# Who asks for an expert's rows: moving 28 row loads from GpSimd to ScalarE's hardware queue

## What is computed

```
scores = sigmoid(t @ w_router); best group of 4; top 2 in it; gates normalised
hidden = silu(t @ w_gate[e]) * (t @ w_up[e])        # per expert e, D_FF 512
out    = sum over the token's 2 experts of gate * (hidden @ w_down[e])
```

## Time and profile before

| | us |
|---|---|
| median of 3 runs | 1522.41 |
| lowest, highest | 1518.6, 1524.04 |
| span of the profiled execution | 1516.7 |
| PE busy in it | 1309.2 (86%) |
| ACT busy in it | 338.1 (22%) |
| POOL busy in it | 165.0 (11%) |

### The profile page before, as it was taken

How to read it: one execution, slowest core, us unless ns; L and a number is a source line. 1 busy time by engine, 2 the same in 40 slices (tenths; PEclk the granted TensorE clock), 3 DMA queues, 4 the chain that set the end, 5 groups by cost and what they waited for, 6 DMA issues and landing times.

```text
span 1516.7 us, 38874 instructions
## 1 busy us (share of the span) xinstructions
PE 1309.2 (86%) x16856; PEld 913.1 (60%) x16856; DVE 521.0 (34%) x1144; ACT 338.1 (22%) x671; POOL 165.0 (11%) x238
## 2 busy tenths in 40 slices
PE   5989999989998988899877669888999888998672
PEld 2448844468888457798444334445664678974441
DVE  1324444145556734011101053457555431111003
ACT  2223221143223131000000033433452300010001
POOL 2003310024333001000000030010000010000001
PEclk8999999999999989899999879987979899999997
DMA  9841159831001175899999882134314469999995
GB/s 397 304 154 59 59 202 314 298 151 59 25 37 58 56 288 195 308 386 395 385 398 415 358 296 89 78 121 173 111 56 167 177 250 331 399 393 399 391 426 191
DMA packets 42105, 354.68 MB, mean 234 GB/s; under 512 B 5707, under 2 KB 10651, under 8 KB 23664
## 3 DMA queue, kind: packets, MB, share of 16 engines
q1 hardware_dynamic: 21456, 302.11, 50.7%
q0 software_dynamic: 8704, 28.53, 5.6%
q10 hardware_dynamic: 11808, 22.03, 4.4%
HBM read 321.63 MB, written 31.01 MB: 233 GB/s over the span
## 4 chain that ended last, share of the span: by engine, by line
PE 65%; DMA 17%; DVE 7%; issue 7%; ACT 3%; POOL 1%; SPq 0%; ACTq 0%; POOLq 0%; DVEq 0%
PE PB L688 59%; DMA arena<-in_w_moe 7%; PE PB L691 6%; DMA ring<-in_w_moe 4%; DVE arena L2010 3%; DMA dispatched<-arena,rows_i 2%; DMA ring<-in_w_mod 2%; ACT arena L1540 1%; DMA arena<-dispatched 1%; DVE small L2023 1%; DMA expert_out<-arena 1%; POOL dispatched L631 1%; DVE arena L2017 1%; DVE x L2010 0%; DVE arena L2014 0%
## 5 line engine op out<-in xcount | busy, mean ns | idle before, releaser
L688 PE MATMUL PB<-arena 64*64 64x64 f32 (+6 forms) x9756 | 489.6, 294 | 48.6 <-DMA arena<-in_w_moe 30.0
L688 PEld LDWEIGHTS PB<-arena 64*64 64x64 f32 (+3 forms) x9756 | 399.8, 129 | 133.9 <-issue 69.7
L688 PE MATMUL PB<-ring,hT 128*128 128x512 f32 (+1 forms) x720 | 313.8, 591 | 7.2 <-DVE hT L2013 3.6
L688 PEld LDWEIGHTS PB<-ring,hT 128*128 128x128 f32 x720 | 137.1, 193 | 167.0 <-issue 162.4
L688 PE MATMUL PB<-ring,arena 128*32 128x256 f32 (+2 forms) x3456 | 195.3, 380 | 33.7 <-DMA ring<-in_w_moe 31.0
L688 PEld LDWEIGHTS PB<-ring,arena 128*32 128x32 f32 x3456 | 147.8, 110 | 73.0 <-issue 24.8
L1540 ACT ACTIVATE arena<-PB 128x256 f32<-128x256 f32 (+3 forms) x217 | 106.6, 491 | 331.1 <-PE PB L688 277.5
L691 PE MATMUL PB<-cst,arena 128*128 128x128 f32 (+2 forms) x758 | 118.6, 298 | 52.3 <-ACT arena L1540 17.9
L691 PEld LDWEIGHTS PB<-cst,arena 128*128 128x128 f32 (+2 forms) x758 | 91.1, 157 | 98.6 <-issue 57.9
L2431 DVE TENSOR_TENSOR arena<-arena,PB 128x256 f32<-128x256 f32 (+1 forms) x32 | 15.1, 471 | 300.9 <-PE PB L688 287.7
L688 PE MATMUL PB<-ring,scT 128*32 128x512 f32 x384 | 60.8, 753 | 21.6 <-DMA ring<-in_w_mod 16.0
(11 more groups left out here) (149 smaller groups left out, 928.9 us busy)
## 6 DMA issues: line engine op xcount, KB each, us to landing
arena<-in_w_moe SPq DMA_DIRECT2D x50, 2048.0 KB, 16.5
ring<-in_w_moe SPq DMA_DIRECT2D x46, 2048.0 KB, 14.5
ring<-in_w_mod SPq DMA_DIRECT2D x24, 2048.0 KB, 8.9
ring<-in_w_mix SPq DMA_DIRECT2D x22, 2048.0 KB, 8.6
dispatched<-gate ACTq DMA_DIRECT2D x1, 8320.0 KB, 50.4
arena<-dispatched POOLq DMA_DIRECT2D x20, 256.0 KB, 9.2
expert_out<-gate ACTq DMA_DIRECT2D x1, 3456.0 KB, 22.1
expert_out<-arena ACTq DMA_DIRECT2D x12, 288.0 KB, 8.7
```

The costliest lines, as they stand in the source:

```text
L688: return nc.tensor.matmul(out, lhsT, rhs, start=start, stop=stop, **k)
```

## The change

GpSimd no longer asks for the experts' rows; its loops at L636 to L644 are gone, and after the scatter its next instruction is the gather behind the stage. ACT asks for them. It waits for `dispatched` after `silu(0)`, asks for the rows of experts 2 and 3, and goes on with `rows_copy(1)`. From then on, the request for expert `c+3` stands right behind `rows_copy(c+1)` and ahead of `store(c-1)`. It has no wait of its own: `rows_copy(c+1)` has waited until PE had turned over the rows of `c+1`, which lay in the same buffer. ACT's first loop (the experts with 96 rows) is written out, which the sizes of the requests need.

```
-                L = base_loop[l]
-                with pool.Fori(1, FULL // 2) as i:
-                    for b in range(2):
-                        pool.wait_ge(*steps_of(L, "xT_p", i, b - 2))
-                        pool.dma_start(xb[0:CAP, b, :], Xd[...CAP rows...]).then_inc(x_land[b], 16)
-                with pool.Fori(FULL // 2, half) as i:
-                    ... the same with SMALL
@@ ACT, experts(l)
                 rows_copy(L, None, 0, 0)
                 nc.scalar.activation(xT[:, 0, 4 * CAP:8 * CAP], PB[:, 1, 0:4 * CAP], ACT.Copy).then_inc(L["S"]["xT_v"], 1)
                 silu(L, None, 0, 0, CAP)
+                def load(b, row, cap):
+                    act.dma_start(xb[0:cap, b, :], Xd[row, :]).then_inc(x_land[b], 16)
+                act.wait_ge(sem("dispatched"), 96 * (l + 1))
+                for b in range(2):
+                    load(b, rows_of(2 + b), CAP)
                 rows_copy(L, None, 1, 1)
                 silu(L, None, 1, 1, CAP)
-                with act.Fori(0, FULL // 2 - 1) as i:
-                    ...
+                for c in range(1, FULL + 1):
+                    rows_copy(L, None, c + 1, (c + 1) % 2)
+                    load((c + 1) % 2, rows_of(c + 3), cap_of(c + 3))
+                    store(L, None, c - 1, (c - 1) % 2, rows_of(c - 1), CAP)
+                    silu(L, None, c + 1, (c + 1) % 2, cap_of(c + 1))
+                with act.Fori(FULL // 2, half - 2) as i:
+                    ... the same, two experts a turn, rows of SMALL
+                for c in (NE - 3, NE - 2):
+                    ... the same without load
```

More of the change, by code:

```diff
@@ L634, in experts @@
                 pool.wait_ge(sem("dispatched"), 96 * (l + 1))
-                L = base_loop[l]
-                with pool.Fori(1, FULL // 2) as i:
-                    for b in range(2):
-                        pool.wait_ge(*steps_of(L, "xT_p", i, b - 2))
-                        pool.dma_start(xb[0:CAP, b, :], Xd[bass.ds(i * 2 * CAP + b * CAP, CAP), :]).then_inc(x_land[b], 16)
-                with pool.Fori(FULL // 2, half) as i:
[L641 to L644, removed]
                 pool.wait_ge(*when("y_all", l))
@@ L1831, in experts, with cap_of, rows_of @@
                 silu(L, None, 0, 0, CAP)
+                def cap_of(c):
+                    return CAP if c < FULL else SMALL
+                def rows_of(c):
+                    at = c * SMALL + min(c, FULL) * (CAP - SMALL)
+                    return slice(at, at + cap_of(c))
+                def load(b, row, cap):
[3 more added lines that the diff above has]
+                    load(b, rows_of(2 + b), CAP)
                 rows_copy(L, None, 1, 1)
                 silu(L, None, 1, 1, CAP)
-                with act.Fori(0, FULL // 2 - 1) as i:
+                for c in range(1, FULL + 1):
[4 more added lines that the diff above has]
+                with act.Fori(FULL // 2, half - 2) as i:
                     for n in (1, 2):
                         rows_copy(L, i, n + 1, (n + 1) % 2)
[L1837 to L1845, removed]
+                        load((n + 1) % 2, bass.ds(i * 2 * SMALL + (n + 3) * SMALL + FULL * GRP, SMALL), SMALL)
                         store(L, i, n - 1, (n - 1) % 2, bass.ds(i * 2 * SMALL + (n - 1) * SMALL + FULL * GRP, SMALL), SMALL)
                         silu(L, i, n + 1, (n + 1) % 2, SMALL)
+                for c in (NE - 3, NE - 2):
+                    rows_copy(L, None, c + 1, (c + 1) % 2)
+                    store(L, None, c - 1, (c - 1) % 2, rows_of(c - 1), SMALL)
+                    silu(L, None, c + 1, (c + 1) % 2, SMALL)
                 for n in (NE - 2, NE - 1):
```

## The result

| | us | ratio to before, 95% interval |
|---|---|---|
| before, median of 5 runs on the same chip (lowest, highest) | 1521.68 (1518.6, 1524.04) | |
| changed, median of 5 runs (lowest, highest) | 1528.87 (1525.32, 1533.54) | 1.0057, 1.0040 to 1.0075 |
| changed, run again beside a later set of before | 1532.42 (before 1518.77) | 1.0101, 1.0070 to 1.0131 |

The change makes the kernel slower, by 7.2 us in the first comparison and 13.7 us in the second, taken between the medians; the ratios in the table stand for 8.7 and 15.3 us. The forecast was 1527.3 us.

The account below looks back on a forecast made before the run. PE (65%) and DMA (17%) both bounded the kernel, with the scatter and first rows' landing on the path. The start's +2.3 and +2.6 us, other terms zero, made +4.9 on 1522.4: 1527.3 us, range 1519 to 1533.

Parts of the forecast that it names:

- The start: At each layer's first experts: rows_copy(1) 8.46 and 8.41 us later, waits of 6.14 and 5.84 gone; net +4.9 us.
- PE's clock: Clock loss moves from rows_T(2) and down(0) to hidden_T(0) and gate_up(1); taken as equal, bound 1 us a layer.
- rival 3: After over 9 us idle, hidden_T(0) and gate_up(1) run longer at 1.2 GHz: 3 us more a layer, 1533 us; chance 0.10.
- The way to the end: From PE's start to the stage's end: SP's weight requests shift equally, so the start's whole delay arrives.
- Rival 2: Absorbed: the weight stream ends the stage and loses only 0.5 to 1 us a layer, 1524 us; chance 0.20.
- The later loads: The other 24 requests, about 0.55 us each, hide in ACT's idle time; stores behind them cost nothing: zero.
- The queue: Rate falls beside row loads come from the 64- or 96-partition destination, so moving them to ACT's queue gains zero.
- rival 1: Faster: the falls are the software queue's and go, saving 12.7 us a layer from 640 to 820, 1502 us; chance 0.12.
- Slower by over 0.3%: Outcome class for the whole kernel, over 4.6 us slower: chance 0.47, against same 0.36 and faster 0.17.

Follow-up runs that it names:

- E1: Kernel before plus ACT's wait for the scatter ahead of rows_copy(1), GpSimd still asking for all rows: 1523.35 us, ratio 1.0012 to before.
- E8: Changed kernel, with SP holding expert 2's up matrix and all weights behind it until the scatter has ended: 1510.67 us, ratio 0.9957 to before.
- E5: Kernel before, unedited, run and profiled a second time: 1515.83 us, ratio 0.9983 to before.
- E6: Changed kernel, unedited, run and profiled a second time: 1532.42 us, ratio 1.0101 to before.
- E10: E7 with expert 3's gate matrix also asked for later, once PE has turned expert 2's rows: 1514.62 us, ratio 0.9974 to before.
- E7: Kernel before, with SP holding expert 2's up matrix and all weights behind it until the scatter has ended: 1507.32 us, ratio 0.9930 to before.
- E9: Kernel before, with expert 3's gate matrix asked for only once PE has turned expert 2's rows: 1515.33 us, ratio 0.9977 to before.
- E4: E2 with small experts' 64 rows sent to partitions 0 to 31 and 64 to 95 by two DMAs: 1527.50 us, ratio 1.0043 to before.
- E3: Kernel before, small experts' 64 rows sent by GpSimd to partitions 0 to 31 and 64 to 95 in two DMAs: 1524.56 us, ratio 1.0023.
- E12: Kernel before, with small experts' 64-row loads reading the input instead of the scattered table, so other rows are computed: 1833.14 us, ratio 1.2068 to before.
- E2: Changed kernel, with the scatter wait and first two row requests moved behind rows_copy(1): 1524.52 us, ratio 1.0024 to before.
- E11: Kernel before, with each small load bringing 128 rows into all partitions instead of 64 into 64: 1506.74 us, ratio 0.9928 to before.

## Why the prediction came out as it did

**The start: right in mechanism and near in size.** rows_copy(1) was put at 608.6 and stands at 609.03, with the DMA of `dispatched` as its releaser; in layer 1 it was put at 1246.0 and stands at 1253.78, in a layer that began 8.1 us later. The waits before rows_T(2) are gone. The net shift was put at 2.3 and 2.6 us; out(0) is 2.1 and 3.3 us later, 5.3 instead of 4.9. E1 splits it. The wait without the requests, by the prediction's terms 8.46 - 1.15 - 6.14 = 1.2 and 1.4 us, moved out(0) by -0.2 and +1.0. The requests, put at 1.15 in each layer, moved rows_copy(1) by 1.1, and out(0) by 2.3 in all, since the clock came back later than in E1. E8 shows that all of it hangs on the length of the scatter. Against E5, whose layer 0 had no wait for the first rows, out(0) of E6 is later by 10.4 and 3.3 us: the prediction took one profile's wait of 6.14 us as given, and it is not.

**PE's clock: right in layer 0, at its bound in layer 1.** The idleness was 13.8 us and not 9, since PE came earlier; in E6, with PE's gaps, it was 8.6 and 8.9 us, as predicted. The granted clock was 0.50 (1.2 GHz) for 3.68 us and 0.78 for the next 4.85, now on hidden_T(0) and gate_up(1): a loss of 1.8 + 1.1 = 2.9 us, as the 3.0 of the earlier trace rows. In layer 1 it was 0.50 for 3.68 us and 0.74 for 4.90, 3.1 us instead of 2.0, about the 1 us that the prediction left open. E6, with its shorter idleness, has the same clocks (0.50 for 3.68 us, then 0.76 for 5.00).

```profile
609.67:613.35 3.68, 3.68 (x34) 3.04 (x37) 0.56 (x1) 0.00 (x0) 0.00 (x0) 0.50 0.67 199
613.35:618.20 4.85, 4.85 (x75) 4.54 (x71) 0.00 (x0) 0.00 (x0) 0.00 (x0) 0.78 0.01 3
```

The idleness was more than twice that of before, and still rival 3's 3 us more in each layer didn't come.

**The way to the end: a term that was missing.** The prediction let SP's requests be late "by the same amount" as PE, and took the 4.9 us whole. But expert 3's gate and up matrices don't follow down(0), where the net shift is 2.1 to 3.3 us. They follow gate_up(1), which stands behind the wait that comes and ahead of the wait that goes, and so is later by the whole 8.5 us and the cold clock, 11 us. In the profiles the stage ends 6.6 and 6.9 us later, of which 2.1 and 3.3 are PE's and 4.6 and 3.7 arise behind out(0); in E6 against E5 the two layers together end 20.2 us later, 13.7 of them at out(0) and 6.5 behind it. The 1.5 MB that the DMA engines didn't carry up to 628 us are worth 3.8 us. Three comparisons speak for it as a cause: E1 (first output -0.2 and +1.0, end 3.4 and 5.4 us later, no row load on ACT), E10 against E7 (first output equal, 0.44% slower in the runs), E9 (first output 8 us earlier, end nearly unmoved). In the runs the whole change costs 7.2 and 13.7 us in its two sets. If out(0) takes 5.3 of them, 2 to 8 us are left behind it, where the prediction had none. The late weights are the main part by these comparisons; a cost of the row loads on ACT's queue may be in it too (E8, E4). That the forecast came within 1.6 us of the first median is partly luck: the term that it lacked happened to be small in that set, and in the second set it is 9 us low.

**Rival 2 had the right limit and the wrong sign.** It said that the weight stream ends the stage; E9 bears that out. But its bound (0.5 us a layer) let the bytes of the first matrices flow at 426 GB/s from 618.9 us on without a break. The stretch from 618 to 628 us moved 308, and 628 to 640 us 366: SP asks for one matrix at a time, 5 us apart, each when PE frees its place. With the start 11 us late the stream had more to make up, not less.

**The later loads: put at zero, about 3 us or nothing, not settled.** ACT's later requests hide, as predicted. PE's waits in layer 0 of the changed kernel, 600 to 878 us, against the earlier trace rows (total, times, longest), name none of the row loads:

```profile
PE PB L678 <- DMA arena<-in_w_moe: 17.5, 9, 3.5
PE PB L681 <- ACT arena L1791: 13.8, 1, 13.8
PE PB L678 <- DMA ring<-in_w_moe: 9.9, 6, 3.2
```

The waits for weights had been put at about 31 us and are 27.4; a PE that runs at 0.89 of its clock in 748 to 808 us, instead of 1.00, needs longer, which fits with shorter waits. The row loads land in 11.9 us instead of 9.2 and are still in time. But the stream may be slower beside them. From 165 to 240 us behind the layer's first rows_copy, every kernel in which GpSimd asks for 64 rows moves 395 to 404 GB/s (before, E1, E3, E5, E7, E9, E10, E12, both layers); with ACT asking it is 386 to 394 in the changed kernel, E2, E4 and E6, but 402 and 399 in E8. With E8's 3.3 us over E7 and E4's 2.9 over E3 that leaves room for a cost of some 3 us, and E8's rate speaks against it.

**The queue: zero, right.** The falls stayed on the hardware queue, down to 244 GB/s, so rival 1 (1502 us) is refuted, and E11 and E12 show what the falls go with. (In the earlier trace rows there are three falls and not four: of the four requests in that window the last stands at 797.75 us, and its rows land behind it. The sum doesn't use this.) The Trainium skill's "SBUF — State Buffer", on the DMA port swizzle, says that partitions 0 to 63 are reached through 8 of the 16 ports; by that rule, the trace agrees: with loads of 64 partitions beside the weights the rate falls to between 244 and 350 GB/s, with 128 it stays at 376 or more. The Trainium skill's "DMA: Bandwidth & Descriptors", in its table of figures, offers crowding by software descriptors only as a best guess for why two of the DMA engines are slow; the prediction's reading of it for these falls, by which they would go on ACT's queue, isn't borne out. Rival 1's price, though, was too high even for a cure: a rate of 427 saved 4.2 us a layer between out(0) and out(15), not 12.7, for E11 improves only the small experts' part and moves more bytes.

**Chances.** "Slower by over 0.3%" had 0.47 and was the outcome in both sets. It should have had more: the prediction itself worked out in its bound for rival 2 that the first matrix is asked for at 617.9 (618.72 was measured, 607.12 before), and then priced the forecast as if that were a delay of 2.4 us.

## What to carry to other kernels

When a wait moves along an engine's list, don't carry only its net shift at the place where the old wait stood: look at each step between the old and the new place, and at what other engines ask for behind it. Here PE's net shift was 2 to 3 us, but the weight requests hung on the steps in between and came 11 us late, on a stage that is bound by those weights. And before putting a request on another queue, ask what makes the transfer slow: here it was what ran beside it (the next weights held back made the scatter 12 us shorter, 0.7%) and how many partitions it fills (128 instead of 64, 0.7%); who asked gained nothing. E7 and E11 touch different places; together they weren't tried.

## What the runs showed of the hardware

- A scatter of six indirect DMAs ended 29.5 us behind the first rows_copy with weights beside it and at 17.6 us without (E7); the last of its requests is made by 14 us in both. DMA of E7, 575.84 to 595.84 us (slices of 0.5 us), and of the kernel before, 578 to 608 us:

```profile
GB/s 0 0 0 0 0 0 0 0 0 33 0 0 0 0 0 0 303 401 344 311 410 328 328 410 311 377 401 328 385 401 352 393 410 98 33 0 0 328 131 229
DMA packets 887, 3.52 MB, mean 176 GB/s; under 512 B 96, under 2 KB 96, under 8 KB 864
```

```profile
DMA packets 1155, 7.39 MB, mean 246 GB/s; under 512 B 128, under 2 KB 128, under 8 KB 896
```

  Alone it runs at 300 to 410 GB/s from about 584 to 592.5 us. With two matrices asked for beside it, 7.4 MB had to pass before it was through.
- The first rows (96 partitions) landed in 4.30 us with no weights beside them (E9) and in 9.62 us with them.
- A load of 64 partitions pulls the total rate from about 430 to between 244 and 350 GB/s for three to four slices of 1.5 us. One of 128 partitions and twice the bytes leaves it at 376 or more.
- PE has short gaps of 0.4 to 0.8 us between 10 and 15 us behind the first rows_copy in some executions and none in others. They shift SP's requests by 4.6 us and so decide whether expert 3's weights meet the scatter. What they come from stays open.
